# Value tiles in one row with the modulation sums behind them, and two weight casts of the output projection moved to earlier attention iterations

## The reference, cut to what matters

```
# layer 0 (even): projections of the same h; the rwkv7 mixer uses r, k, v, wd, ad
mod = silu(c) @ ada_w[l] + ada_b[l]              # per layer: shift, scale, gate
h = rms_norm(x, norm_g[l]) * (1 + scale) + shift
z = h @ even_w_in
a_val, a_glu, a_gate, r, k, v, wd, ad, b_gate = split_cols(z, EVEN_SIZES)
v = v + (token_shift(v) - v) * mu                # a "value tile": 128 columns of v
...
# layer 1 (odd): top-k sparse attention with 16 heads, then a gate and a projection
o = dsa_attention(q, k, v, qi, ki, wi, positions)
out = (o * silu(g)) @ odd_w_out
x = x + gate * out
```

## Time and profile before

| what | us |
|---|---|
| median of 3 runs | 2064.54 |
| lowest, highest | 2062.06, 2065.65 |
| the profiled execution's own time | 2063.91 |
| its span in the profile | 2062.2 |
| TensorE busy | 1956.5 (95%) |
| DVE busy | 1427.8 (69%) |
| ACT busy | 996.5 (48%) |

### The profile page before, as it was taken

How to read it: one execution, slowest core, us unless ns; L and a number is a source line. 1 busy time by engine, 2 the same in 40 slices (tenths; PEclk the granted TensorE clock), 3 DMA queues, 4 the chain that set the end, 5 groups by cost and what they waited for, 6 DMA issues and landing times. The chain is left out here.

```text
span 2062.2 us, 29832 instructions
## 1 busy us (share of the span) xinstructions
PE 1956.5 (95%) x12519; PEld 1774.0 (86%) x12519; DVE 1427.8 (69%) x1720; ACT 996.5 (48%) x1137; POOL 79.3 (4%) x123
## 2 busy tenths in 40 slices
PE   5987899999999999999999899999999999999998
PEld 4866778878887968999999798989898989898976
DVE  6787897354766346566446588888888888787862
ACT  2511111215366313443445476667666666666654
POOL 3000000000000100100220000000000000000000
PEclk8998999998999999999999999999999999999999
DMA  9845121344242432456662388989898999998980
GB/s 332 265 143 174 52 83 62 123 158 170 93 153 82 166 123 82 125 183 206 183 224 101 123 300 325 350 326 352 328 349 329 349 330 345 333 344 333 349 305 21
DMA packets 225857, 452.29 MB, mean 219 GB/s; under 512 B 6944, under 2 KB 91176, under 8 KB 225720
## 3 DMA queue, kind: packets, MB, share of 16 engines
q1 hardware_dynamic: 222400, 445.44, 61.7%
q0 software_dynamic: 1632, 4.75, 0.9%
q10 hardware_dynamic: 1688, 0.15, 0.1%
HBM read 448.21 MB, written 2.10 MB: 218 GB/s over the span
## 5 line engine op out<-in xcount | busy, mean ns | idle before, releaser
L2003 DVE TENSOR_TENSOR ring_r<-ring,his_r 128x2816 fp32r<-128x2816 f32 (+1 forms) x192 | 586.9, 3085 | 61.5 <-ACT his_r L1543 61.3
L1543 ACT ACTIVATE his_r<-ring 128x2816 fp32r<-128x2816 f32 (+1 forms) x192 | 490.9, 2560 | 199.6 <-DMA ring<-in_moe_w_dram 189.9
L1149 PE MATMUL bank<-his_r,hg_r 128*128 128x352 f32 x2048 | 356.4, 326 | 0.8 <-ACT hg_r L1567 0.8
L1149 PEld LDWEIGHTS bank<-his_r,hg_r 128*128 128x128 f32 x2048 | 334.1, 188 | 1.8 <-issue 0.9
L2476 PE MATMUL bank<-hT,ring 128*128 128x256 f32 x912 | 214.8, 392 | 4.0 <-DVE arena L3054 2.2
L2476 PEld LDWEIGHTS bank<-hT,ring 128*128 128x128 f32 x912 | 175.1, 196 | 32.4 <-issue 8.0
L1149 PE MATMUL bank<-ring_r,hg_r 128*128 128x352 f32 x1024 | 185.9, 323 | 0.0
L1149 PEld LDWEIGHTS bank<-ring_r,hg_r 128*128 128x128 f32 x1024 | 169.0, 188 | 0.0
L3075 DVE SCALAR_TENSOR_TENSOR arena<-ring,cw,arena 128x256 f32<-128x256 f32 x240 | 96.5, 476 | 0.1
L1175 PE MATMUL bank<-his_r,at_hi_r 128*128 128x512 f32 x352 | 93.8, 399 | 0.0
L1175 PE MATMUL bank<-his_r,at_lo_r 128*128 128x512 f32 x352 | 92.5, 396 | 0.0
(11 more groups left out here) (541 smaller groups left out, 2938.7 us busy)
## 6 DMA issues: line engine op xcount, KB each, us to landing
ring<-in_moe_w_dram SPq DMA_DIRECT2D x128, 1408.0 KB, 8.4
ring<-in_moe_w_dram SPq DMA_DIRECT2D x48, 1536.0 KB, 9.0
ring<-in_even_w_in_dram SPq DMA_DIRECT2D x28, 1024.0 KB, 5.9
ring<-in_ffn_w_dram SPq DMA_DIRECT2D x22, 1024.0 KB, 5.4
ring<-in_ada_w_dram SPq DMA_DIRECT2D x20, 1024.0 KB, 10.0
ring<-in_odd_w_in_dram SPq DMA_DIRECT2D x9, 2048.0 KB, 7.7
ring<-in_moe_w_dram SPq DMA_DIRECT2D x16, 1024.0 KB, 6.9
ring<-in_a_w_in_dram SPq DMA_DIRECT2D x6, 2048.0 KB, 8.1
```

The source lines that it names most:

```text
L1149: ins = mm(bank[first + m][:, 0:WC], x[:, KT // 2 * late + k, :], w[:, k, WC * m:WC * m + WC], start=(not late and k == 0 and s == "hg_hi" ...
L1543: A(moe_hi(n), moe_w(n), ACT.Copy).then_inc(sem("moe_hi"), 1)
L2003: V.tensor_tensor(moe_lo(n), moe_w(n), moe_hi(n).bitcast(F32), ALU.subtract).then_inc(sem("moe_lo"), 1)
```

## The change

Three edits in the even layer and two in the attention:

- TensorE's `ada(8)` and `ada(9)`, which stood behind value tiles 4 and 5, now stand behind tile 7.
- DVE's `modulation(0, 16, 24)` and `modulation(1, 0, 16)`, which stood ahead of `value(7)`, now stand behind it, with a wait for `ada_summed` of 10.
- ACT's `oo_cast(0)` and `oo_cast(1)` move from iterations 13 and 15 to iterations 9 and 11.
- DVE's `oo_low(0)` moves from iteration 14 to iteration 10, and `oo_low(1)` from behind the attention to iteration 12.
- The lists of counts are reordered to match.

```
-        OO_HI = ["x0", "x1", "x2", "x3", "x4", "w0", "x5", "w1", "x6", "x7"] + [f"w{q}" for q in range(2, 8)]
-        OO_LO = ["x0", "x1", "x2", "x3", "x4", "w0", "x5", "x6", "x7"] + [f"w{q}" for q in range(1, 8)]
+        OO_HI = ["x0", "x1", "x2", "w0", "x3", "w1", "x4", "x5", "x6", "x7"] + [f"w{q}" for q in range(2, 8)]
+        OO_LO = ["x0", "x1", "x2", "w0", "x3", "w1", "x4", "x5", "x6", "x7"] + [f"w{q}" for q in range(2, 8)]
...
                 if b >= 4 and b % 2 == 0:
                     gated_hi(b // 2 - 2)
-                elif b >= 13:
-                    oo_cast((b - 13) // 2)
+                elif b in (9, 11):
+                    oo_cast((b - 9) // 2)
...
                 if b >= 5 and b % 2 == 1:
                     gated_lo((b - 5) // 2)
-                elif b == 14:
-                    oo_low(0)
+                elif b in (10, 12):
+                    oo_low((b - 10) // 2)
...
             gated_lo(7)
-            oo_low(1)
...
                 z("zV", q)
                 if q < 2:
                     tok(4 + q)
-                elif q in (4, 5):
-                    ada(4 + q)
+            ada(8)
+            ada(9)
             pe.wait_ge(sem("mod_ready"), 3)
...
                 elif q == 6:
                     glu_used(0)
                     conv(4)
-                    modulation(0, 16, 24)
-                    modulation(1, 0, 16)
+            dve.wait_ge(sem("ada_summed"), 10)
+            modulation(0, 16, 24)
+            modulation(1, 0, 16)
             br_masks(0, 0, 4)
```

## The result

The changed kernel takes 2053.6 us (median of 6 runs, 2052.92 to 2056.15) against 2064.14 (6 runs, 2062.06 to 2065.65) for the kernel before: 10.5 us less, a ratio of 0.995 with an interval of 0.994 to 0.996. 2050 was forecast, with a range of 2046 to 2056, so the time lies inside the range, 3.6 us above the forecast.

A forecast was written before the change was run, and what follows sets the result against it. TensorE was taken as the bound, busy 1956.5 of 2062.2 us, so only its stops or clock count. Value tiles 12.6 plus casts 1.6 gave 14.2 us off 2063.91, 2049.7; 2050 was forecast, range 2046 to 2056.

The forecast's parts named there:

- tile 4 to `br_pair`: Value tiles: with tiles 5 to 7 in a row, `br_pair` starts at 200.4 instead of 213.28, gaining 12.9 us.
- `br_pair` to L2560 (clock): Behind the value tiles: a clock fall within the second half of `br_pair` costs 0 to 1.2 us, 0.3 chosen.
- attention: Moved casts: 4.2 us late mid-attention, shorter tail at full clock, projection at 659.8 instead of 661.43; gain 1.6 us.
- Tiles 5 to 7 as a row of 10.5 us: Sign in the profile after: the three value tiles run as one row from 186.75, both sums behind it.
- `br_pair` at 200.4: Sign at the end of the value-tile stretch: `br_pair` starts near 200.4; later than 204 makes the prediction wrong.
- second rival: Value tiles: the row runs at half clock, 10.4 + 1.6 = 12.0 us gained, so 2052.5; chance 9%.
- gate tile 13 waits: Sign in the attention: gate tile 13 waits 1.6 us for ACT's copy, which the moved cast delays.
- the prediction's own mark: Wrong if `turned` (transposes) of iteration 11 to the projection is not about 6 us shorter than before's 24.3.
- first rival: Moved casts lose: the clock falls in mid attention, 12.6 - 1.4 = 11.2 us gained, so 2053; chance 12%.
- Gain lost later: Later in the even layer something that did not move sets the pace; 12.6 is waited off, 2063; chance 6%.
- part two: Attention: casts and remainders moved from the tail to earlier iterations; gain 1.6 us, both ends 5.8 and -1.4.
- the two clock rivals: Clock falls in mid attention (2053, 12%), or the row of value tiles runs at half clock (2052.5, 9%).

The follow-up runs named there:

- experiment 7: Changed kernel plus 8 unread dense products in TensorE's stops around `br_pair`: 2050.07 us, ratio 0.9928.
- experiment 8: Changed kernel with the casts in iterations 7 and 11 and the remainders in 8 and 12: 2050.95 us, ratio 0.9934.
- experiment 2: Kernel before with only the casts and remainders moved, as in the change; value tiles left as they were: 2063.99 us, ratio 0.9996.
- experiment 9's third run: Changed kernel with only tile 0 of the next attention's beta, C and H products moved into the 2.77 us stop: 2051.00 us, ratio 0.9933.
- its last: Changed kernel plus dense fill around `br_pair`, casts in 7 and 11, remainders in 8 and 12, and tile 0 in the 2.77 us stop: 2043.61 us.
- experiment 4: Changed kernel with only the remainders moved, to iterations 12 and 14; casts stay in 9 and 11: 2055.00 us, ratio 0.9953.
- experiment 3: Changed kernel with the casts in iterations 7 and 11 and the remainders in 12 and 14: 2053.47 us, ratio 0.9947.
- experiments 1 and 6: 1: changed kernel with casts and remainders put back as before, 2054.56 us. 6: changed kernel with `ada(8)` behind value tile 6, 2053.96 us.
- the second of 9: Changed kernel plus four unread dense products in TensorE's stop ahead of the transposes of iteration 11: 2053.80 us, ratio 0.9946.
- the first of 9: Changed kernel plus dense fill around `br_pair`, casts in iterations 7 and 11, remainders in 8 and 12: 2048.82 us, ratio 0.9921.
- experiment 5: The changed kernel run once more, unaltered, for a second trace: 2052.45 us, ratio 0.9940 to the kernel before.

## Why the prediction was right, and where it was 4 us too good

The account of the profiled executions, all from starts of instructions in the two traces:

| stretch | forecast | measured |
|---|---|---|
| start to tile 4 | 0 | -1.08 |
| tile 4 to `br_pair` | +12.9 | +13.12 |
| `br_pair` to L2560 (clock) | -0.3 | -2.19 |
| L2560 to first gate tile | 0 | -0.55 |
| attention | +1.6 | -0.02 |
| projection to the end | 0 | +0.32 |
| sum | 14.2 | 9.60 |

- Tiles 5 to 7 as a row of 10.5 us: 10.60. `br_pair` at 200.4: 201.24, of which 1.08 was late already ahead of the changed place. The step was right to 0.3 us. Both sums took 1.84 us at full clock, as summed.
- The clock behind it, 0.3, bounds 0 to 1.2: 2.19, outside the bounds. This is the step that failed most: "the fall can come within the second half of `br_pair` ... choose 0.3 since the first half and its mask pass first". They didn't. The fall came in the first half (+0.5), the second ran wholly at 1.2 GHz (+0.9), and so did more of the w products (+0.8), which the bound had left out. Every trace with the row shows the fall in the first half, and experiment 7 shows that dense products in the stops give most of it back. That the row of tiles fell to half clock was the second rival, 9%; tiles 5 to 7 ran at 1.00 in all twelve traces that have no sums behind tiles 4 and 5 (the row took 10.60 us in ten of them), and only tile 4 ahead of them fell, in one (experiment 8).
- The attention: gate tile 13 waits 1.54 (1.6 forecast), the transposes of iteration 11 wait 2.18 (2.5) and are 3.98 late (4.2), the tail runs at 1.00. With the clock held the stretch is 101.3 in three traces, 1.6 under before, the term to the tenth. In the changed kernel's own traces the clock takes these 1.6 us back. From those transposes to the projection it is 20.3 us, 4.0 shorter than before's 24.3 and not about 6: by the prediction's own mark, this step was wrong, and for the reason that its first rival gave. (With the clock held, in experiment 2, it is 18.7 us, 5.6 shorter.)
- Loss ahead of the attention, 0.55: not forecast. It is the clock alone: over this stretch TensorE is idle for 16.78 us in both traces and busy for 315.23 us instead of 314.67. The same stop of 2.2 us ahead of the second `br_pair` was followed by 1.16 us before and by 2.08 after, and other places gave some back (the gain stood at 9.85 us at L2560, 9.86 at that pair, 8.31 at 388 us, 9.28 at 473 and 9.30 at the first gate tile):

```profile
320.83 1.16 PE L2541 MATMUL bank<-arena 64*128 64x128 f32 x16 [2.24 <-DVE arena L3174]
```

```profile
310.97 2.08 PE L2540 MATMUL bank<-arena 64*128 64x128 f32 x16 [2.23 <-DVE arena L3173]
```

- The start, 1.08 us: tile 4 began between 180.63 and 183.09 in the fourteen traces, whose kernels are the same up to there. It is the spread of executions.
- The rest: the gain at the projection (9.28) reaches the end (9.60). "Gain lost later" was wrong.

The first rival, a drop in mid attention, was what happened in part two; I gave it 12%. I had weighed it by tile 4 between its two stops, one case, against it. That row could not carry so much. In the kernel before, the second of these stops goes on to 4.76 us, so the row says nothing of the work behind two short stops; and in experiment 8 tile 4, at the same place, did fall to half clock. The measured 2053.6 lies nearer to the two clock rivals (2053 and 2052.5) than to the forecast: the range held because it took them in, and the likeliest case was not what happened. The Trainium skill, TensorE: Matmul & The Clock Gate, section "A second HAM failure mode: psum-queue depth-cycling", has the clock swing between its two levels where TensorE idles shortly between groups of products. The trace of the changed kernel agrees, with 1.6 us; that of experiment 2, with the same stops, does not, so here it is a risk and not a rule.

## What to carry to other kernels

Taking a stop away is worth its length only if the clock behind it stays where it was: after the sum of the waits, look for the next gapped stretch and price it at half clock, all of it, not only its second half. Where a stop can't be closed, put real work that stands behind it into it. That gave the stop in experiment 9's third run and both the stop and the clock in its last. And before an edit is placed "where there is room", look for what else stands in that iteration on that engine: the cast in iteration 9 made the transposes of iteration 11 1.8 us late (experiment 4), the same cast two iterations earlier nothing (experiment 3). In iteration 9 ACT works without a stop from the Silu's table load (617.07) to the copy of the gate tile (625.43); in iteration 7 it had stood idle for 2.65 us.

## What the runs showed of the hardware

The same stop is followed by a lower clock in one execution and not in another. Ahead of the second logits of the next attention TensorE stands 2.77 us in both kernels. The changed kernel, and then the one of experiment 8, whose stop comes 6.2 us earlier:

```profile
752.24 0.70 PE L876 MATMUL bank<-arena 64*128 64x256 f32 x4 [2.77 <-DVE arena L1837]
752.87 7.17 PE L867 MATMUL bank<-hT,ring 128*128 128x256 f32 x32
```

```profile
746.01 1.22 PE L876 MATMUL bank<-arena 64*128 64x256 f32 x4 [2.77 <-DVE arena L1837]
747.17 9.72 PE L867 MATMUL bank<-hT,ring 128*128 128x256 f32 x32
```

That costs 3.1 us in one trace, nothing in the other, and it hid most of what experiment 8 had won. Twelve traces have this stop. From the second logits to the third it is 7.95 or 7.96 us in five of them (before, both of the changed kernel, experiments 1 and 6), 9.6 in five (experiments 2, 3, 4, 7 and the second of 9), and 11.0 in two (8 and the first of 9). The moment, counted from the start of the execution, does not decide it by itself: the second logits began at 752.24 in the changed kernel without a drop and at 752.29 in the second run of experiment 9 with one.

Such drops, 0.9 to 3.1 us each, at stops of 1.1 to 2.8 us, are as large as the edits of this case. The changed kernel's two traces repeat them (experiment 5); no other kernel has two. So an edit early in a kernel can gain or lose microseconds hundreds of microseconds later, without any change there. What decides was not settled; no run varied the time of a stop alone.
